# Out-projection inside the RWKV stage: seven block products in place of eight, evicted by VectorE; gate product at the stage's end

## The reference, cut to what matters

```python
h = rms_norm(x, norm_mix[l]); proj = h @ w_in[l]
y_s5, y_lru, y_ssd = ...                       # three mixers of 512 columns
# rwkv7: a recurrence over 512 tokens, 8 heads of 64
g = jax.nn.sigmoid(xg) @ g2                    # 96 x 512: the gate product
o = ((o - mean) * lax.rsqrt(var + RW_LN_EPS)).reshape(bsz, s, RW_W)
o = o * ln_w + ln_b
y_rw = (o + bonus) * g
mixed = jnp.concatenate([y_s5, y_lru, y_rw, y_ssd], axis=-1)   # 512 x 2048
x = x + mixed @ w_out[l]                       # 512 x 2048 x 2048
h = rms_norm(x, norm_ffn[l])
x = x + hier_moe(h, ...)                       # 64 experts, 2 of them for a token
return rms_norm(x, norm_final)
```

## Time and profile before

| | |
|---|---|
| median of 3 runs | 2401.31 us (2400.78 to 2402.77) |
| the profiled execution | 2401.06 us |
| its span, first to last instruction | 2398.8 us |
| PE busy | 2225.1 us, 93% |
| DVE busy | 788.0 us, 33% |
| ACT busy | 448.3 us, 19% |
| POOL busy | 401.1 us, 17% |
| DMA read and written | 753.23 MB and 47.19 MB |

### The profile page before, as it was taken

One profiled execution on the slowest core, in us unless ns is written; L12 is line 12 of the kernel. 1 busy time (PEld: TensorE's weight loads), 2 busy tenths in 40 slices (PEclk: granted clock), 3 DMA queues, 4 the chain that ended last, 5 costly groups with the idle time before them and its releaser, 6 DMA issues.

```text
span 2398.8 us, 33897 instructions
## 1 busy us (share of the span) xinstructions
PE 2225.1 (93%) x13339; PEld 1248.6 (52%) x13339; DVE 788.0 (33%) x1289; ACT 448.3 (19%) x788; POOL 401.1 (17%) x589
## 2 busy tenths in 40 slices
PE   8999999999999999999998888898888888888887
PEld 4577778885555456444444444344443444434443
DVE  6799684356333314111111111111111111111114
ACT  3544352115222221000000000000000000000002
POOL 4022223331422001111111111101011111111110
PEclk9999999999999999999999999999999999999999
DMA  6588869873321466999999999999999999999998
GB/s 191 115 171 181 184 135 215 168 162 108 99 81 56 141 272 258 411 428 424 426 427 424 427 426 425 428 425 426 428 424 429 425 426 427 425 426 427 424 426 366
DMA packets 237801, 760.83 MB, mean 317 GB/s; under 512 B 36024, under 2 KB 173564, under 8 KB 193948
## 3 DMA queue, kind: packets, MB, share of 16 engines
q1 hardware_dynamic: 174008, 710.29, 73.9%
q0 software_dynamic: 54016, 42.00, 9.7%
q10 hardware_dynamic: 9700, 7.45, 1.0%
HBM read 753.23 MB, written 47.19 MB: 334 GB/s over the span
## 4 chain that ended last, share of the span: by engine, by line
PE 50%; DMA 42%; DVE 7%; issue 1%; ACT 0%; ACTq 0%; DVEq 0%; SPq 0%; POOL 0%; POOLq 0%
DMA big<-in_moe_w 40%; PE ps L3045 12%; PE ps L2689 11%; PE ps L2756 7%; PE ps L3076 4%; DVE big L1546 3%; PE ps L2656 3%; PE ps L2922 2%; DMA big<-in_norm_final 1%; PE ps L3061 1%; PE ps L2843 1%; PE ps L3029 1%; PE ps L2823 1%; PE ps L2704 1%; DVE big L1700 1%
## 5 line engine op out<-in xcount | busy, mean ns | idle before, releaser
L3045 PE MATMUL ps<-big 128*64 128x384 f32 x4096 | 697.1, 495 | 93.8 <-DMA big<-in_moe_w 83.6
L3045 PEld LDWEIGHTS ps<-big 128*64 128x64 f32 x4096 | 298.7, 139 | 498.5 <-issue 364.7
L3076 PE MATMUL ps<-big 128*64 128x512 f32 x1536 | 390.9, 664 | 51.0 <-DVE big L2378 51.0
L2689 PE MATMUL ps<-big 128*128 128x256 f32 x1792 | 393.8, 380 | 2.6 <-DVE big L1678 2.6
L2689 PEld LDWEIGHTS ps<-big 128*128 128x128 f32 x1792 | 338.6, 190 | 60.5 <-issue 12.5
L2374 DVE TENSOR_SCALAR big<-ps,scal 128x384 f32<-128x384 f32 x64 | 39.6, 618 | 690.8 <-PE ps L3045 690.8
L3076 PEld LDWEIGHTS ps<-big 128*64 128x64 f32 x1536 | 115.5, 151 | 279.5 <-issue 219.0
L2383 DVE SCALAR_TENSOR_TENSOR big<-ps,scal,big 128x512 f32<-128x512 f32 x128 | 90.2, 747 | 397.8 <-PE ps L3076 397.8
L1463 ACT ACTIVATE big<-ps,scal 128x384 f32<-128x384 f32 x64 | 37.2, 581 | 793.7 <-PE ps L3045 769.0
L1033 POOL COPY scal<-slots 128x3 f32 (+1 forms) x64 | 11.9, 187 | 907.4 <-DVE big L2383 892.1
L2756 PE MATMUL ps<-big 128*128 128x512 f32 x320 | 153.5, 610 | 0.9 <-ACT big L1216 0.7
(11 more groups left out here) (446 smaller groups left out, 1780.8 us busy)
## 6 DMA issues: line engine op xcount, KB each, us to landing
big<-in_moe_w SPq DMA_DIRECT2D x187, 3072.0 KB, 38.4
big<-in_w_in SPq DMA_DIRECT2D x96, 512.0 KB, 4.8
big<-in_w_in POOLq DMA_DIRECT2D x32, 512.0 KB, 7.9
big<-big POOLq DMA_DIRECT2D x16, 512.0 KB, 5.1
big<-in_w_out SPq DMA_DIRECT2D x8, 1024.0 KB, 5.5
big<-y_rows SPq DMA_DIRECT2D x8, 1024.0 KB, 27.9
big<-in_moe_w SPq DMA_DIRECT2D x4, 1536.0 KB, 23.4
big<-in_x SPq DMA_DIRECT2D x4, 1024.0 KB, 8.4
```

The costliest lines, as they stand in the source:

```text
L2689: last = nc.tensor.matmul(o, w[:, k, :], side[:, k, :], start=(k == 0 and b in (0, 1, 5)), stop=(k == 7), skip_group_check=True)
L3045: last = nc.tensor.matmul(ps[2 + w][B * g:B * g + B, 0:FF], xT[k][:, j, B * g:B * g + B], W13[k][w][:, NJ * g + j, :], start=(j == 0), sto ...
L3076: last = nc.tensor.matmul(ps[5 + q][B * g:B * g + B, :], hid[k][:, m, :], W2[k][:, m, 512 * n:512 * n + 512], start=(m == 0), stop=(m == F ...
```

## The change

The product of the 1536 finished columns of `mixed` with `w_out` (512 x 1536 x 2048) is cut by two in all three directions: halves of 256 tokens, of 768 rows of `w_out` and of 1024 columns, and the eight block products are replaced by seven, as in the in-projection. The columns go in four groups of 256 (`g`); a piece is one block product of a group: 12 matmuls with a moving side of 256 columns into one bank, two token tiles by six row blocks. There are 28 pieces, 336 matmuls of half the width. Products 0, 2, 4, 6 of a group run on in bank 7, products 5, 1, 3 in bank 6, and each is evicted before the next is added to its bank.

- Weights: each piece has a tile of 768 KB in one of four slots. SP loads its first block when the piece four before it is complete; POOL adds the others with accumulating DMAs (17 in all, from HBM or from another slot), each after the load before it has landed.
- The other side: POOL makes four differences of token halves in front of the stage (12 subtractions of 128x512), DVE the last (four operations in the first pair).
- Eviction: the first three pieces by ACT (and POOL adds them to x), the other 25 by DVE in one operation that adds them onto `xpart`.
- `share`: 48 matmuls before the first chunk, 48 for each pair (2, 10, 6, then 4 behind `t` and 2 behind `u`), 36 in the chains, 12 behind `mean`, 48 behind `var`.
- The gate product (four matmuls of 512 columns) moves from before `prep` to between the pieces of `mean` and the `var` blocks.
- TensorE waits for the eviction of the in-projection's last product before the LoRA products, where it waited at the first piece.

```diff
...
+        wo_slot = [big[:, 62:65, :].rearrange("p a n -> p (a n)"), big[:, 65:68, :].rearrange("p a n -> p (a n)"), small[:, 0:1536],
+                   big[:, 68:71, :].rearrange("p a n -> p (a n)")]
+        wo_slot = [x.rearrange("p (c n) -> p c n", c=6) for x in wo_slot]
...
+        mix_in = [[Y5[:, 0:2], Y5[:, 2:4], YL[:, 0:2]], [YL[:, 2:4], Z_[:, 0:2], Z_[:, 2:4]]]
+        O11, O12, O21, O22 = ([x[:, :, TO * t:TO * t + TO] for x in mix_in[k]] for k in range(2) for t in range(2))
+        OT1 = [two(big[:, i, :]) for i in (92, 93, 94)]
+        OT2 = [two(big[:, i, :]) for i in (16, 17, 19)]
+        OT3 = O12
+        OT4 = [two(big[:, 95, :]), two(big[:, 56, :])]
+        OT4_LAST = [small[:, 1536:1792], big[:, 18, 256:512]]
+
+        def wo_side(b, c):
+
+            if b == 6 and c >= 4:
+                return OT4_LAST[c - 4]
+            return (O11, OT1, OT2, O22, OT3, O21, OT4)[b][c // 2][:, c % 2]
...
-        for m in range(16):
-            plan(("po", m), m if m < 2 else 7)
+        OB = [(0, b) for b in (5, 0, 1, 3, 2, 4, 6)] + [(g, b) for g in range(1, 4) for b in (5, 0, 1, 2, 3, 4, 6)]
+        OB_AT = {x: m for m, x in enumerate(OB)}
+        OB_LAST = {}
+        for g in range(4):
+            for q, bs in enumerate(((5, 0), (6,), (2, 3), (1, 4))):
+                OB_LAST[max([OB_AT[g, b] for b in bs] + [3] * (g == 0))] = q
+        OB_PAIRS = 20
+        NOB = len(OB)
+        OB_TO = {5: (0, 0, 1), 0: (0, 0, 1), 1: (1, 1, -1), 2: (1, 0, 1), 3: (1, 0, 1), 4: (1, 1, -1), 6: (0, 1, -1)}
+        OB_SUM = {0: ["A11"], 1: ["A22", "A21"], 2: ["A11", "S1"], 3: ["A12", "S2"], 4: ["A21", "A11"], 5: ["A12"], 6: ["A22"]}
+
+        def ob_sum(m):
+
+            g, b = OB[m]
+            return ["A12", "A11", "S1"] if m == OB_AT[0, 3] else OB_SUM[b]
+
+        for m, (g, b) in enumerate(OB):
+            plan(("po", m), 7 if b % 2 == 0 else 6)
...
-        share = [(("prep", 0), 6), (("prep", 1), 6), (("prep", 2), 12)]
-        sizes = itertools.cycle([1, 5, 4] + [2, 2] * (LEV - 1))
+        share = [(("prep", 0), 12), (("prep", 1), 12), (("prep", 2), 24)]
+        sizes = itertools.cycle([2, 10, 6] + [4, 2] * (LEV - 1))
...
-        share += [(("chain", c, step), 3) for c in (NRC - 2, NRC - 1) for step in range(3)]
-        share += [(("mean",), 6), (("var",), 24)]
+        share += [(("chain", c, step), 6) for c in (NRC - 2, NRC - 1) for step in range(3)]
+        share += [(("mean",), 12), (("var",), 48)]
...
+        def wo_step(eng, start, m, j):
+
+            g, b = OB[m]
+            name = ob_sum(m)[j]
+            if j:
+                eng.wait_ge(*WO_IN[m][j - 1])
+                s_, z = WO_IN[m][j]
+                eng.wait_ge(s_, z - 16)
+            kw = {"accum_op": ALU.add} if j else {}
+            if name[0] == "S":
+                n = OB_AT[g, int(name[1])]
+                eng.wait_ge(*WO_IN[n][-1])
+                start(wo_slot[m % 4], wo_slot[n % 4], **kw).then_inc(WO_IN[m][j][0], 16)
+            else:
+                c0 = 1024 * (int(name[1]) - 1) + 256 * g
+                for a, z, to in WO_K[int(name[2])]:
+                    start(wo_slot[m % 4][:, to:to + z - a, :], wov[:, a:z, c0:c0 + 256], **kw).then_inc(WO_IN[m][j][0], 16)
...
+        ACC_AT = {}
+        for g in range(1, 4):
+            for a, p in enumerate((-1, 0, 1, 2)):
+                ACC_AT[7 * g + p] = (7 * g + 2 + a, 1)
...
+            def piece(m):
+
+                g, b = OB[m]
+                k, i = at[("po", m)]
+                sp.wait_ge(full[k], i + 1)
+                if m + 4 < NOB:
+                    wo_load(m + 4)
+                if m - 1 in OB_LAST and OB[m - 1][0] < 3:
+                    x_load(OB_LAST[m - 1], OB[m - 1][0] + 1)
+                if m in OB_LAST and m != NOB - 1:
+                    q = OB_LAST[m]
+                    if m == 3:
+                        sp.wait_ge(padd_ok, 5)
+                    else:
+                        sp.wait_ge(free[k], i + 1)
+                    sp.dma_start(x_quad(q, g, x2d), xpart[q].rearrange("p (i c) -> p i c", i=2)).then_inc(x_io[q], 16)
...
+            pool.wait_ge(prod_ok, PROD + PB_ * NF)
+            pool.wait_ge(away_in, AWAY_IN + 32)
+            pool.wait_ge(mix_ok, 12)
+            for c in range(3):
+                side_op(OT1[c], O11[c], O12[c], sub, 1 if c == 2 else False)
+            accumulate(2, 1)
+            pool.wait_ge(dec_ok, 3)
+            for c in range(3):
+                side_op(OT2[c], O12[c], O22[c], sub)
+            accumulate(3, 1)
+            g.settle()
+            for c in range(3):
+                side_op(OT2[c], OT2[c], O11[c], sub, 2 if c == 2 else False)
+            accumulate(3, 2)
+            g.settle()
+            for c in range(3):
+                side_op(OT3[c], O22[c], OT3[c], sub, 3 if c == 2 else False)
+            accumulate(4, 1)
+            accumulate(5, 1)
...
-                take(("lora", q, 2), Gt[:, q, :])
...
+                    if m < 3:
+                        take(("po", m), early[m], scale=float(OB_TO[OB[m][1]][2]))
...
+            def out_part(where):
+
+                for m in ends[where]:
+                    if m < 3:
+                        continue
+                    g, b = OB[m]
+                    t, n, sign = OB_TO[b]
+                    q = 2 * t + n
+                    src, done = got(("po", m))
+                    dve.wait_ge(x_io[q], X_AT[g])
+                    if g == 0 and q == 3:
+                        dve.wait_ge(padd_ok, 6)
+                    to, a, z = xpart[q], src[:], xpart[q]
+                    if m == NOB - 1:
+                        dve.wait_ge(ro_ok, NRC)
+                        to = big[:, 40:48, :].rearrange("p a n -> p (a n)").rearrange("p (i d) -> p i d", i=2)[:, :, 1792:2048]
+                        a, z = (x.rearrange("p (i c) -> p i c", i=2) for x in (a, z))
+                    v.tell(nc.vector.scalar_tensor_tensor(out=to, in0=a, scalar=float(sign), in1=z, op0=MUL, op1=ADD), *done)
+                    v.settle()
...
+            out_part(("mean",))
             dve.wait_ge(var_ok, VAR_OK + WT)
             for q in range(WT):
-                v.do(nc.vector.scalar_tensor_tensor(out=Ot[:, q, :], in0=Ot[:, q, :], scalar=A("rw_ln_w", q), in1=wk[:, q, :], op0=MUL, op1=MUL))
+                v.do(nc.vector.scalar_tensor_tensor(out=Ot[:, q, :], in0=Ot[:, q, :], scalar=A("rw_ln_w", q), in1=wk[:, 4 + q, :], op0=MUL, op1=MUL))
             v.settle()
             dve.wait_ge(bv_ok, WT)
             for q in range(WT):
                 v.do(nc.vector.scalar_tensor_tensor(out=Ot[:, q, :], in0=Ot[:, q, :], scalar=A("rw_ln_b", q), in1=BV[:, q, :], op0=ADD, op1=ADD))
             v.settle()
             for q in range(WT):
-                v.tell(nc.vector.tensor_tensor(V_[:, q, :], Ot[:, q, :], Gt[:, q, :], MUL), rwy_ok, q + 1)
+                b, i = at[("lora", q, 2)]
+                dve.wait_ge(free[b], i + 1)
+                v.tell(nc.vector.tensor_tensor(V_[:, q, :], Ot[:, q, :], Gt[q], MUL), rwy_ok, q + 1)
+            out_part(("var",))
...
+                    m, r = divmod(at_, PO)
+                    i, c = divmod(r, 6)
+                    g, b = OB[m]
+                    o, k = at[("po", m)]
+                    if r == 0:
+                        if m == 0:
+                            pe.wait_ge(mix_ok, 12)
+                            pe.wait_ge(away_in, AWAY_IN + 32)
+                        pe.wait_ge(free[o], k)
+                        pe.wait_ge(*wo_summed(m))
+                        if g == 0 and b in (1, 2, 4):
+                            pe.wait_ge(padd_ok, {1: 1, 2: 2, 4: 3}[b])
+                        if g == 0 and b == 6:
+                            pe.wait_ge(side_ok, SIDES + 2)
+                    last = nc.tensor.matmul(ps[o][:, TO * i:TO * i + TO], wo_side(b, c)[:, P * i:P * i + P], wo_slot[m % 4][:, c, :],
+                                            start=(r == 0 and b in (0, 1, 5)), stop=(c == 5), skip_group_check=True)
+                    if r == PO - 1:
+                        last.then_inc(full[o], 1)
...
-            for q in range(WT):
-                o, done = fill(("lora", q, 2))
-                nc.tensor.matmul(o[:], loraW[:, 1, P * q:P * q + P], LO[:, 1, :], start=True, stop=True).then_inc(done, 1)
...
             blocks64("mean", Ot)
             out_part(("mean",))
+            pe.wait_ge(gates_in, 48 + 64)
+            for q in range(WT):
+                o, done = fill(("lora", q, 2))
+                nc.tensor.matmul(o[:], loraG[:, P * q:P * q + P], LO[:, 1, :], start=True, stop=True).then_inc(done, 1)
             blocks64("var", mixd, cen_ok)
             out_part(("var",))
...
```

More of the change, by code:

```diff
@@ L135, in build @@
         loraW = big[:, 84:86, :]
+        loraG = big[:, 85, :]
         s5C = big[:, 86:88, :].rearrange("p r (g c) -> p r g c", g=NPAIR)
@@ L350, in build @@
                     plan(("tm", c, k), 4 + k)
-                plan(("gram", c, 0), 6)
```

(52 more changed lines are left out.)

231 lines of the change are left out of this document (117 added, 114 removed).

## The result

The changed kernel takes 2415.3 us (median of 4 runs, 2412.5 to 2417.7) where the kernel before takes 2401.05 beside it (2399.5 to 2402.8): a ratio of 1.0059, 95% interval 1.0041 to 1.0076. It is slower by 14 us. The prediction said 2402.3 with a range of 2394 to 2412, and was wrong. The profiled execution took 2415.27 us with a span of 2413.5, against 2398.8 before: 14.7 us more.

What follows compares the result with a forecast made beforehand. TensorE was taken to bound the RWKV stage's pairs, and stage changes to reach the end one for one through the weight stream. 10.5 - 19 + 9.5 = +1.0; 2401.06 + 1.0 + 0.25 = 2402.3 us, range 2394 to 2412.

Steps and rivals of the forecast that it cites:

- Before the first chunk: Ahead of `rw_pre`: VectorE and GpSimd take turns and piece 3 waits for three DMAs in a row, +10.5 us.
- Price of a matmul and of the pairs' work: Half-width matmuls cost half, 0.432 us against 0.86: 20.6 us less, all in the four pairs, 5.1 a pair.
- The pairs: Four pairs of chunks: 20.6 us less TensorE work, about 1.6 back in small waits, together -19 us.
- step (a): Second `gram`, first pair: eviction and subtractions take VectorE about 4.2 us after the piece, so TensorE waits 0.8 once.
- I take 0, as the spacing is the nearer row: In the pairs, GpSimd's wait on landings before its masks costs 0; 4 x 1.3 us if each dependent sum is late.
- rival B: Pairs bound by latency: GpSimd stands at a landing while `rw_t` waits for its mask; +11 us, 2412, chance 0.23.
- The gate product: At the stage's end, four matmuls between two parts of a dependent chain, hidden by nothing: +3.4 us.
- The stage's end: From `mean` to `out_rw`: bank wait 4.7, gate product 3.4, clock after idle 1.2; written as +9.5 us.
- The bank and VectorE's list: Behind the `var` blocks, piece 26 waits for VectorE's eviction of piece 24 from bank 7 until V + 15.1: +4.7 us.
- What stands behind the stage: Second norm, router and experts keep their order, later `x2` and expert loads stay hidden: 0 us.

Runs made afterwards that it cites:

- the last run: Changed kernel with VectorE's three `rw_first` subtractions placed ahead of the eviction behind the second `gram`: single execution, wait 3.51 us, first pair 41.5 us in place of 38.9.

## Why the prediction was wrong, point by point

**Before the first chunk: right.** +10.5 forecast, +11.7 measured, by the causes it gave, each seen: VectorE's chain to 608.66 (609 forecast), piece 3's last sum at 603.2 (604.6), the low clock behind the wait (8.15 us for 5.45 of work, 2.7 where 1 to 1.7 was put). The early sum and the longer low clock largely cancel, which is luck. The Trainium skill's rule ("SBUF — State Buffer", section "SBUF: two separate sides") agrees with the trace in both directions: 4.39 us more beside 4.28 of subtractions, and nothing more beside memsets, which read nothing.

**Price of a matmul and of the pairs' work: right.** 5.1 us less for each pair is what the second and third pair show once their waits are gone.

**The pairs: the first failed step.** -19 forecast, -12.0 measured. Of the 8.6 us that were lost from the 20.6, the first pair lost 3.1, the second 4.0, the third 1.1, the fourth 0.3. The first pair's is step (a), put at 0.8: TensorE waited 2.32 at the place named. VectorE needed 5.9 us from the piece's end, where 4.2 was put, because the three subtractions were priced "without POOL beside them": they took 3.2 in place of 1.26. GpSimd does work beside them in the first pair: it adds the first three pieces onto x. The second pair's is the wait of 1.96 for instructions and 1.5 us of low clock behind it. "I take 0, as the spacing is the nearer row" failed here, though not as rival B had it: no wait for POOL's masks shows in the changed kernel. What came late beside the sums was not GpSimd but, by the reading above, TensorE's own instructions, a cost for which the sum had no term; in the run without sums it is gone. How a sum delays them stays open.

**The gate product: right.** +3.4 and +3.6.

**The stage's end: the second failed step.** +5.9 forecast, +10.2 measured. The bank and VectorE's list were read rightly (V + 13.7 for V + 15.1, once the transfers are out of the way), but they aren't what comes last. The sum counted banks and evictions and never asked when pieces 24 to 27 have their weights; it took sums as landing in time here too. The trace of before had the rows for it, not used: the router's weights kept SyncE for 12.7 us, harmlessly, since no load of a piece stood behind them.

```profile
791.56 12.70 SPq L699 DMA_DIRECT2D big<-in_moe_w_expert  x1
```

And the 4 MB load had 14.7 us from issue to landing. The change puts four loads and three dependent sums behind both.

**What stands behind the stage: within the scatter.** +1.3; from `out_rw` to the end the profiled executions of kernels that leave this part and the loads for it alone lie between 1557.8 and 1559.7 us (with memsets for the differences 1561.6; where the 4 MB or the router's weights move, 1558.0 to 1563.8).

**The balance.** +1.0 forecast against +14.7: 7.0 missed in the pairs, 4.3 at the end, 1.2 at the start, 1.3 behind the stage. Of the 11.3 of the first two, the run without sums gives 7.8 back, 2.9 in the pairs and 4.9 at the end. The rest of its 11.2 lies at the start (2.1) and behind the stage (1.2), where executions scatter by as much. What it doesn't give back is the first pair. The prediction knew late transfers only as rival B, with a price for the pairs alone.

## What to carry to other kernels

When a change adds a load that something waits for, walk through the issuing queue and write down what stands ahead of it, its time to issue and its bytes, and do the sum for the last transfers as for the last banks. A transfer that is moved away from one user lands on the next: it must be put where nothing that others wait for is under way. And an engine's spare time next to VectorE is not spare if its operations read SBUF there: twelve subtractions made VectorE's chain end 11.9 us later, and moving nine of them, with piece 3, into the first pair took 6.7 us off the kernel. Finally, a wait of TensorE without a releaser is worth a look at the transfers of its instructions.

## What the runs showed of the hardware that I had not expected

- A load of 768 KB took 5.8 us in the changed kernel, some 18 behind 4 MB of its own queue (twice), and an accumulating one 18 us behind 4 MB of another engine's queue. In the first of these the DMA engines' share from 790 to 810 us was 1.07, at 352 GB/s. The Trainium skill's "DMA: Bandwidth & Descriptors", section "Queues, rings and completion order", says that a completion's increment lands only after every earlier write of that DMA engine, across its queues; these numbers agree with it. Whether it is that or the shared bandwidth the runs don't tell apart.
- Waits of TensorE that I read as waits for its own instructions: up to 1.96 us, each ending 1.29 to 1.63 us behind a 16 KB transfer of the kind `instruction`, in every trace but that of the kernel without sums.
- Issuing the router's expert weights, 512 KB in rows of 256 bytes, held SyncE for 8.1 to 17.0 us (12.7 before); issuing the 4 MB held it for 0.4 to 1.1.
- Accumulating sums of 768 KB took 7.6, 8.8 and 10.5 us in a row at the end, against 5.1 and 7.9 for 512 KB before.
- TensorE's clock. Busy time of the changed kernel in two stretches (the granted clock is the first value behind the brackets):

```profile
620.00:630.00 10.00, 7.47 (x125) 5.76 (x127) 7.80 (x12) 0.00 (x0) 7.58 (x8) 1.00 0.57 187
670.00:680.00 10.00, 8.04 (x160) 6.44 (x156) 2.67 (x7) 1.80 (x6) 4.26 (x5) 0.83 0.82 181
```

In the first, with an idle time of 2.32 us, the clock stays at its upper level of 2.4 GHz; with 3.51 idle in the same stretch (the last run) the mean is 0.83, and twelve records take 4.54 us in place of 2.86. But in the second it is 0.83 too, after an idle time of 1.96 only. The length of one wait doesn't tell it.
